# First norm of a decoder kernel by halves of the tokens, with weights ahead of x's second half, two tiles on the first half first, and the small vectors on ScalarE's queue

## What is computed

```python
def rms_norm(x, gain):
    xf = x.astype(jnp.float32)
    y = xf * lax.rsqrt(jnp.mean(xf * xf, axis=-1, keepdims=True) + NORM_EPS)
    return (y * gain.astype(jnp.float32)).astype(x.dtype)
...
h = rms_norm(x, mix_norm[layer])
...
q, k, v, g = jnp.split(h @ w_in, [H * dk, 2 * H * dk, 2 * H * dk + H * dv], axis=-1)
q = apply_rope(q.reshape(B, S, H, dk), positions)
k = apply_rope(k.reshape(B, S, H, dk), positions) * (dk ** -0.5)
```

## Time and profile before

| | us |
|---|---|
| median of 3 runs | 2768.65 (2768.4 to 2768.74) |
| the profiled execution, its device time | 2771.12 |
| span of its profile | 2769.2 |
| TensorE busy in the span | 2699.9 |
| VectorE / ScalarE / GpSimd busy | 1357.4 / 827.0 / 1268.4 |
| TensorE busy in the first 38 us | 20.77 |

### The profile page before, as it was taken

One profiled execution on the slowest core, in us unless ns is written; L12 is line 12 of the kernel. 1 busy time (PEld: TensorE's weight loads), 2 busy tenths in 40 slices (PEclk: granted clock), 3 DMA queues, 4 the chain that ended last, 5 costly groups with the idle time before them and its releaser, 6 DMA issues.

```text
span 2769.2 us, 35757 instructions
## 1 busy us (share of the span) xinstructions
PE 2699.9 (97%) x12145; PEld 2237.2 (81%) x12145; DVE 1357.4 (49%) x1866; ACT 827.0 (30%) x1404; POOL 1268.4 (46%) x1215
## 2 busy tenths in 40 slices
PE   7999999999999899999999999999988999999998
PEld 6888888888888788888888788787876888888886
DVE  7423423432334764454545537355577444545455
ACT  4220210120023523333323524324265222222223
POOL 3323323323322555665555445253445555655553
PEclk9999999999999999999999999999999999999999
DMA  3102102101111111111121111111111111111211
GB/s 134 39 31 65 42 31 66 46 31 58 50 35 46 33 59 49 53 45 49 53 64 53 31 50 47 31 58 39 47 50 33 56 53 53 45 45 56 65 53 76
DMA packets 173483, 140.03 MB, mean 51 GB/s; under 512 B 8657, under 2 KB 142929, under 8 KB 173393
## 3 DMA queue, kind: packets, MB, share of 16 engines
q1 hardware_dynamic: 171664, 133.53, 15.6%
q10 hardware_dynamic: 1728, 5.26, 0.5%
HBM read 133.51 MB, written 5.24 MB: 50 GB/s over the span
## 4 chain that ended last, share of the span: by engine, by line
PE 91%; DVE 5%; ACT 2%; issue 1%; DMA 0%; POOL 0%; POOLq 0%; SPq 0%; DVEq 0%; ACTq 0%
PE ps L690 30%; PE ps L694 30%; PE ps L693 30%; DVE uc L1940 1%; PE ps L894 0%; PE ps L776 0%; DVE residual L1596 0%; DVE residual L1853 0%; DVE residual L2011 0%; DVE f_h_lo L1736 0%; DVE gate_buf L1945 0%; DVE xn L1552 0%; DVE h_sum_a L1725 0%; DVE uc L1935 0%; ACT L1465 0%
## 5 line engine op out<-in xcount | busy, mean ns | idle before, releaser
L527 POOL TENSOR_TENSOR f_w_lo<-f_raw,f_w_hi 128x512 fp32r<-128x512 f32 x262 | 340.7, 1303 | 434.4 <-ACT f_w_hi L1240 434.3
L690 PE MATMUL ps<-f_h_hi,f_w_hi 128*128 128x512 f32 x1232 | 483.2, 392 | 17.9 <-DVE f_h_lo L1725 12.1
L693 PE MATMUL ps<-f_h_lo,f_w_hi 128*128 128x512 f32 x1232 | 481.5, 391 | 0.0
L694 PE MATMUL ps<-f_h_hi,f_w_lo 128*128 128x512 f32 x1232 | 481.3, 391 | 0.0
L487 POOL TENSOR_TENSOR small<-w_raw 128x1 f32<-128x1 f32 x200 | 55.1, 275 | 845.2 <-PE ps L690 830.0
L1853 DVE TENSOR_TENSOR residual<-ps,residual 128x512 f32<-128x512 f32 x352 | 239.3, 692 | 160.0 <-PE ps L694 160.0
L690 PEld LDWEIGHTS ps<-f_h_hi,f_w_hi 128*128 128x128 f32 x1232 | 232.6, 189 | 70.0 <-issue 15.9
L1240 ACT ACTIVATE f_w_hi<-f_raw 128x512 fp32r<-128x512 f32 x262 | 164.4, 629 | 367.0 <-PE ps L694 349.6
L694 PEld LDWEIGHTS ps<-f_h_hi,f_w_lo 128*128 128x128 f32 x1232 | 232.6, 189 | 48.7
L693 PEld LDWEIGHTS ps<-f_h_lo,f_w_hi 128*128 128x128 f32 x1232 | 232.7, 189 | 48.1
L690 PE MATMUL ps<-f_w_hi,f_act_hi 128*128 128x512 f32 x688 | 268.0, 389 | 3.2 <-POOL f_last_lo L527 3.2
(11 more groups left out here) (261 smaller groups left out, 4773.9 us busy)
## 6 DMA issues: line engine op xcount, KB each, us to landing
f_raw<-in_ffn_w_gu SPq DMA_DIRECT2D x176, 256.0 KB, 3.4
w_raw<-in_ret_w_in SPq DMA_DIRECT2D x96, 256.0 KB, 2.8
f_raw<-in_ffn_w_down SPq DMA_DIRECT2D x88, 256.0 KB, 2.7
w_raw<-in_lru_w_in SPq DMA_DIRECT2D x48, 256.0 KB, 2.9
w_raw<-in_ret_w_out SPq DMA_DIRECT2D x32, 256.0 KB, 2.6
w_raw<-in_lru_w_out SPq DMA_DIRECT2D x24, 256.0 KB, 2.6
residual<-in_x SPq DMA_DIRECT2D x8, 512.0 KB, 6.6
out_y<-residual SPq DMA_DIRECT2D x8, 512.0 KB, 2.6
```

Of the source, the lines that this page charges most:

```text
L527: nc.gpsimd.tensor_tensor(lo, src, hi.bitcast(F32), ALU.subtract).then_inc(f_wready, 1)
L690: m = nc.tensor.matmul(o, l_hi, r_hi, start=start, stop=False, skip_group_check=onto)
L693: nc.tensor.matmul(o, l_hi, r_lo, start=False, stop=False, skip_group_check=onto)
L694: return nc.tensor.matmul(o, l_lo, r_hi, start=False, stop=stop, skip_group_check=onto)
```

## The change

The first norm gets functions of its own on each engine (`first_norm` on ScalarE and VectorE, `first_tiles` on TensorE). The other norms keep theirs, apart from renamed helpers.

- SP loads blocks 0 to 3 of x, the first three weight units (tile 0 and tile 1, features 0 to 511, then tile 0, features 512 to 1023), then blocks 4 to 7, positions and frequencies, then the rest.
- The seven small vectors are issued from ScalarE's queue, after a first square root on a dummy operand, which loads the table.
- The fourth weight unit is split into a buffer of its own, `w4_hi` and `w4_lo`, so POOL does not wait for a place in the ring.
- TensorE first transposes the small vectors. Then it works by halves of the tokens: transposes of k = 0 to 3 of the first half, then products of tiles 0 and 1 on it, with the transposes of k = 4 to 7 in between; then the same for the second half. Products of a tile and half go to bank tile + 2 * hf, transposes use banks 4 to 7.
- ScalarE and VectorE follow this order; VectorE scales blocks 0, 1, 2 and 4, 5, 6 for the lower features and 0, 1 and 4, 5 for the upper ones, ScalarE the others.

```diff
-            for s in range(SB):
-                sp.dma_start(X[:, s * D:(s + 1) * D], x[0, s * P:(s + 1) * P, :]).then_inc(x_in[s], 16)
-            vec = scr[:, 8 * 1024:8 * 1024 + P]
-            for at, n, src in ((C_MIX, 16, mix_norm.rearrange("l (k p) -> (l k) p", p=P)),
-                               (C_FFN, 16, ffn_norm.rearrange("l (k p) -> (l k) p", p=P)),
-                               (C_CONV, 48, lru_conv_w[0].rearrange("j (k p) -> (j k) p", p=P)),
-                               (C_CONVB, 12, lru_conv_b[0].rearrange("(k p) -> k p", p=P)),
-                               (C_BR, 12, lru_b_r[0].rearrange("b c -> (b c)").rearrange("(k p) -> k p", p=P)),
-                               (C_BI, 12, lru_b_i[0].rearrange("b c -> (b c)").rearrange("(k p) -> k p", p=P)),
-                               (C_LAM, 12, lru_lambda[0].rearrange("(k p) -> k p", p=P))):
-                sp.dma_start(vec[at:at + n, :], src).then_inc(vec_in, 16)
-            sp.dma_start(pos[:], positions.to_broadcast([P, S])).then_inc(pos_in, 16)
-            sp.dma_start(invf[:], inv_freq).then_inc(pos_in, 16)
-
+            def x_blocks(first, end):
+                for s in range(first, end):
+                    sp.dma_start(X[:, s * D:(s + 1) * D], x[0, s * P:(s + 1) * P, :]).then_inc(x_in[s], 16)
+            x_blocks(0, 4)
             def load(slot, src, ready):
...
+                    if first and j == RING:
+                        x_blocks(4, SB)
+                        sp.dma_start(pos[:], positions.to_broadcast([P, S])).then_inc(pos_in, 16)
+                        sp.dma_start(invf[:], inv_freq).then_inc(pos_in, 16)
                     if j < 8:
-                        tile, kh = j // 2, j % 2
+
+                        tile, kh = (j % 2, j // 2) if first and j < 4 else (j // 2, j % 2)
                         src = rows(ret_w_in[0], kh, (tile // 2) * D + h * DK + (tile % 2) * P)
...
-                    used = None if first and j < RING else u if j < 2 else u - 1
+                    used = None if first and j <= RING else u if j < 2 else u - 1
+                    if first and j == RING:
+                        place = w4_hi[:], w4_lo[:]
...
+            def first_tiles(u0):
+                e0 = JB_NORM[0]
+                def transposes(hf, ks):
+                    for k in ks:
+                        i = hf * KT + k
+                        if i >= 4:
+                            pe.wait_ge(psum_free, e0 + i - 3)
+                        if k % 4 == 0:
+                            pe.wait_ge(xn_dve, hf * 5 + (3 if k == 0 else 5))
+                            pe.wait_ge(xn_act, hf * 3 + (1 if k == 0 else 3))
+                        for s in range(4):
+                            c = (hf * 4 + s) * D + k * P
+                            m = nc.tensor.transpose(bank(4 + i % 4, s * P, P), xn[:, c:c + P], ident[:])
+                        m.then_inc(psum_full, 1)
+                def products(hf, j, kks=range(4)):
+                    tile, kh = j % 2, j // 2
+                    if hf == 0:
+                        pe.wait_ge(w_ready, u0 + j + 1)
+                    for kk in kks:
+                        k = kh * 4 + kk
+                        if tile == 0:
+                            pe.wait_ge(psum_free, e0 + hf * KT + k + 1)
+                        r = slice(k * S + hf * 512, k * S + (hf + 1) * 512)
+                        if j < RING:
+                            w = slice(j * 512 + kk * P, j * 512 + (kk + 1) * P)
+                            w_h, w_l = w_hi[:, w], w_lo[:, w]
+                        else:
+                            w_h, w_l = w4_hi[:, kk * P:(kk + 1) * P], w4_lo[:, kk * P:(kk + 1) * P]
+                        m = three(bank(tile + 2 * hf), w_h, w_l, h_hi[:, r], h_lo[:, r],
+                                  k == 0, k == KT - 1, hf == 1 and kk == 0)
+                        if hf and k == KT - 1:
+                            m.then_inc(psum_full, 2)
+                pe.wait_ge(ident_ready, 2)
+                pe.wait_ge(vec_in, 16 * 7)
+                nc.tensor.transpose(ps[:, 0:P], scr[:, 8 * 1024:8 * 1024 + P], ident[:]).then_inc(vec_T, 1)
+                transposes(0, range(4))
+                products(0, 0)
+                products(0, 1, (0, 1))
+                transposes(0, range(4, 8))
+                products(0, 1, (2, 3))
+                products(0, 2)
+                products(0, 3, (0,))
+                transposes(1, range(4))
+                products(0, 3, (1, 2, 3))
+                products(1, 0)
+                products(1, 1, (0, 1))
+                transposes(1, range(4, 8))
+                products(1, 1, (2, 3))
+                products(1, 2)
+                products(1, 3)
...
+            def first_norm():
+                def square(s):
+                    act.wait_ge(x_in[s], 16)
+                    square_rows(s, 0)
+                def scaled(s, half):
+                    c = s * D + half * 512
+                    nc.scalar.activation(xn[:, c:c + 512], X[:, c:c + 512], ACT.Copy,
+                                         scale=rstd[:, s:s + 1]).then_inc(xn_act, 1)
+                def upper(hf, ks):
+                    for k in ks:
+                        i = hf * KT + k
+                        full(JB_NORM[0] + i)
+                        nc.scalar.activation(h_hi[:, k * S + hf * 512:k * S + (hf + 1) * 512], bank(4 + i % 4),
+                                             ACT.Copy, scale=cols[:, C_MIX + k:C_MIX + k + 1]).then_inc(h_rounded, 1)
+                act.wait_ge(ident_ready, 2)
+                load_sqrt()
+                vec = scr[:, 8 * 1024:8 * 1024 + P]
+                for at, n, src in ((C_MIX, 16, mix_norm.rearrange("l (k p) -> (l k) p", p=P)),
+                                   (C_FFN, 16, ffn_norm.rearrange("l (k p) -> (l k) p", p=P)),
+                                   (C_CONV, 48, lru_conv_w[0].rearrange("j (k p) -> (j k) p", p=P)),
+                                   (C_CONVB, 12, lru_conv_b[0].rearrange("(k p) -> k p", p=P)),
+                                   (C_BR, 12, lru_b_r[0].rearrange("b c -> (b c)").rearrange("(k p) -> k p", p=P)),
+                                   (C_BI, 12, lru_b_i[0].rearrange("b c -> (b c)").rearrange("(k p) -> k p", p=P)),
+                                   (C_LAM, 12, lru_lambda[0].rearrange("(k p) -> k p", p=P))):
+                    act.dma_start(vec[at:at + n, :], src).then_inc(vec_in, 16)
+                for s in range(4):
+                    square(s)
+                root(0, 4, 1)
+                act.wait_ge(n_rstd, 1)
+                scaled(3, 0)
+                act.wait_ge(cols_ready, 1)
+                upper(0, (0, 1))
+                square(4)
+                upper(0, (2, 3))
+                scaled(2, 1)
+                scaled(3, 1)
+                square(5)
+                upper(0, (4,))
+                square(6)
+                upper(0, (5,))
+                square(7)
+                upper(0, (6, 7))
+                root(4, SB, 2)
+                act.wait_ge(n_rstd, 2)
+                scaled(7, 0)
+                upper(1, range(4))
+                scaled(6, 1)
+                scaled(7, 1)
+                upper(1, range(4, 8))
+            first_norm()
...
+            def first_norm():
+                def square(s):
+                    dve.wait_ge(x_in[s], 16)
+                    c = s * D + 512
+                    STT(scr[:, 2048 + s * 512:2048 + (s + 1) * 512], X[:, c:c + 512], 1.0, X[:, c:c + 512],
+                        ALU.mult, ALU.mult, accum_out=ssq[:, 8 + s:9 + s]).then_inc(n_sq_dve, 1)
+                def scaled(s, half):
+                    c = s * D + half * 512
+                    TS(xn[:, c:c + 512], X[:, c:c + 512], rstd[:, s:s + 1], None, ALU.mult).then_inc(xn_dve, 1)
+                def lower(hf, ks):
+                    for k in ks:
+                        i = hf * KT + k
+                        c = slice(k * S + hf * 512, k * S + (hf + 1) * 512)
+                        dve.wait_ge(h_rounded, i + 1)
+                        STT(h_lo[:, c], bank(4 + i % 4), cols[:, C_MIX + k:C_MIX + k + 1], h_hi[:, c].bitcast(F32),
+                            ALU.mult, ALU.subtract).then_inc(psum_free, 1)
+                for s in range(4):
+                    square(s)
+                inverse_root(0, 0, 4, 1)
+                for s in range(3):
+                    scaled(s, 0)
+                dve.wait_ge(vec_T, 1)
+                nc.vector.tensor_copy(cols[:], ps[:, 0:P]).then_inc(cols_ready, 1)
+                dve.wait_ge(cols_ready, 1)
+                lower(0, (0, 1))
+                square(4)
+                lower(0, (2, 3))
+                scaled(0, 1)
+                scaled(1, 1)
+                square(5)
+                lower(0, (4,))
+                square(6)
+                lower(0, (5,))
+                square(7)
+                lower(0, (6, 7))
+                inverse_root(0, 4, SB, 2)
```

(8 more changed lines are left out.)

84 lines of the change are left out of this document (30 added, 54 removed).

## The result

| | before | after |
|---|---|---|
| median of nine runs each, us | 2770.15 (2768.4 to 2771.55) | 2776.11 (2774.84 to 2779.2) |
| ratio, 95% interval | | 1.0023 (1.0015 to 1.0032) |
| profiled execution, device time (span) | 2771.12 (2769.2) | 2774.87 (2773.0) |

The change costs 6.0 us by the medians (4.2 to 8.9 by the interval), against a forecast of 3.1. The 2776.1 us lies inside the range given (2766 to 2776.5), but by the bound of 5.5 us that the prediction set between "same" and "slower" it is just "slower", and not clearly, since the interval reaches from 4.2 to 8.9. So the traces can explain 3.8 of the 6.0 us.

A forecast was written before the change was run, and what follows sets the result against it. TensorE, busy 97% of the span, was taken to bound the kernel, with VectorE's chain level at the first gate unit. VectorE's 1.6 us plus 1.5 us of slow clock gave +3.1 us, forecast 2771.8 us, range 2766 to 2776.5.

The forecast's parts named there:

- same: Outcome class for the total time: within 5.5 us (0.2%), what a measurement can tell from no change; chance 0.73.
- slower: Outcome class for the total time: more than 5.5 us lost; chance 0.21, from three quarters of C and 0.08 of the forecast.
- The mechanism: First gate unit: TensorE, 7.5 us ahead, waits 6.5 us for VectorE's later freeing of banks; chance 0.60.
- VectorE's chain: Rope tables to second rope pair: start +1.0, one more split +1.3, first pair -0.7; last bank freed 1.6 us later.
- The early table load: ScalarE's root in the first norm: load hidden, scaling starts at 9.9 in place of 10.93, 1.0 us won.
- Rival C, late small vectors: Start of first norm: vectors land at 14.4, TensorE's first instruction waits 3.2 us, total 2775.0 us; chance 0.17.
- A, level: Rival at the first gate unit: nothing lost, last bank freed within 1 us of today's, 2768.0 to 2769.6; chance 0.17.
- B, VectorE does not bind: Rival at the first gate unit: TensorE keeps its 7.5 us lead less 1 us of waits, 2762.2 us; chance 0.06.
- The first norm on TensorE: First transposes at 11.25, last four groups at 35.45, tile 1 ends at 44.0, TensorE some 7.5 us ahead.
- slow start: TensorE's first instructions in the first norm: slow pace until about 16.4, costing 2.6 us (bounds 1.8 and 4.2).
- The clock: Clock of 0.50 after TensorE's wait at the first gate unit, costing 1.5 us (bounds 0 and 3.4).
- Sum: Whole kernel: 1.6 us of VectorE's lateness plus 1.5 us of slow clock, +3.1 us; forecast 2771.8 us.

The follow-up runs named there:

- a_short: Changed kernel without the coarse pass of the angle reduction, 6 of the 17 rope table instructions; 2769.13 us, ratio 0.9994 to the kernel before.
- b_short: Kernel before without the coarse pass of the angle reduction, 6 of the 17 rope table instructions; 2770.97 us, ratio 1.0000 to the kernel before.
- b_vec: Kernel before with only the early table load and the small vectors from ScalarE's queue; 2770.44 us, ratio 0.9999 to the kernel before.
- a_xfirst: Changed kernel with all of x issued ahead of the weights in SP's queue; 2780.14 us, ratio 1.0033 to the kernel before.
- a_hold: Changed kernel with POOL's first split held until VectorE's three first scalings are done; 2775.27 us, ratio 1.0018 to the kernel before.
- a_splits: Changed kernel with weight units 4 and 5 split early into own buffers, VectorE waiting for tile 2 behind the tables; 2773.66 us, ratio 1.0013 to before.
- a_early: Changed kernel with the second-half transposes of k = 4 to 7 moved ahead of more products; 2775.73 us, ratio 1.0016 to the kernel before.
- a_early_mix: Changed kernel with a_early's order of transposes and seven table instructions moved into VectorE's idle places; 2765.75 us, ratio 0.9986 to the kernel before.
- a_best: Changed kernel with a_hold, a_splits, a_early and five table instructions moved into VectorE's idle places; 2766.97 us, ratio 0.9989 to the kernel before.
- a_warm: Changed kernel with six repeats of three matmuls in TensorE's wait at the first gate unit; 2775.71 us, ratio 1.0019 to the kernel before.

## Why the prediction was right or wrong

**The mechanism held.** The forecast said that TensorE would be some 7.5 us ahead and give all of it back at the bank that VectorE frees, because VectorE's chain would be later, not earlier. TensorE was 6.9 us ahead at the gate unit (66.39 against 73.27), waited 7.2 us there (1.36 + 0.39 + 4.66 + 0.74; forecast 6.5 in one piece), and VectorE's last freeing instruction ended 2.86 us later. The first 1.75 us are for banks of the first rope pair, which the forecast had free in time. a_short and b_short show that this chain, and not another, sets the end.

**The early table load: right in kind, half in size.** The load is hidden, as said. Scaling starts at 10.35, 0.58 earlier than before and not 1.0: block 3 of x landed 0.44 us later (8.79 against 8.35). The forecast costed the small vectors at nothing and kept the landing at 8.35. The other traces tell most of the cause. b_vec and a_xfirst, with the seven vectors on ScalarE's queue but all of x ahead of the weights, have block 3 at 8.63 and 8.62; b_short, with neither, at 8.27; after and its other variants, with both, at 8.64 to 8.83. So some 0.3 us came with the vectors and at most 0.2 with the weights.

**Rival C, late small vectors, is refuted.** They landed by 9.54, 4.6 us after the last of their issues was done (4.57 + 0.39), and TensorE then waited for the scalings until 12.70. *A, level*, fell with the 2.86 us, and *B, VectorE does not bind*, with the 4.66 us wait. The Trainium skill (DMA: Bandwidth & Descriptors, "Issuing engines are not separate DMA queues") has transfers of different issuers interleave; this landing, in the middle of x's, agrees.

**The first norm on TensorE: 0.6 us too short.** Full transposes start at 12.70, not 11.25. Of the 1.45 us, 1.0 is the split beside the scalings (shown by a_hold; the forecast took 0.5 later in the sum) and 0.45 the landing. The slow start cost less than taken (about 2 us by the starts of the first transposes and products, an estimate; forecast 2.6), so tile 3 ended at 66.39 against 65.8, and the last transposes ran at 35.97 against 35.45.

**VectorE's chain: the step that failed.** The forecast had +1.0 - 0.7 + 1.3 = +1.6; the trace has +2.86. The tables start 1.66 us later (39.97 against 38.31), 0.67 more than taken. The first pair takes 10.07 us, 1.5 less than before (11.57), where 0.7 less was taken. And the tables take 23.3 us, not 21.9. This last is the term that was mis-sized. Its price per split was near: 23.3 less 15.5 of undisturbed work is 7.8 us, for six splits 1.3 each. (The 15.5 adds up durations; by the distance from start to start, 1.26 us for the long ones and about 0.74 for the others, undisturbed work is 16.2, and a split costs 1.1 us before, 1.2 here, and 1.4 in a_splits and a_early.) The count was wrong: I moved the splits earlier and arrived at five. The first of the six starts at 39.63, just as the tables do, since TensorE had run ahead and released it, and the last at 61.38. Two more splits, not one: +2.7, not +1.3. Taking three out gave 1.0 us each (a_splits). The count alone does not settle it, though: in a_early the tables met five and took 23.05 us, 2.5 more than before. Which instructions a split lies beside counts as well, and the two were not separated. What the count missed is in the starts: the first three are 2.7 us apart (39.63, 42.34, 45.06), the others 5.44. A place in the ring comes free when TensorE begins a unit, and by halves it reuses the four units of tiles 0 and 1 in a second pass, where a unit lasts four products, 12 x 0.227 = 2.7 us. So the splits were not only earlier but also closer together, and just at the tables' start.

**The clock: half of what was taken.** 0.50 came as said, from 74.9 to 81.7, but most of it lay in the wait. Its cost was 0.8 us (lag 3.60 against 2.80 with the clock kept up), where I took 1.5 with bounds of 0 and 3.4. The Trainium skill (TensorE: Matmul & The Clock Gate, "Terms") would price the stretch at half of itself, 3.4 us; the runs show less, since the time in which TensorE waits anyway costs nothing at any clock.

**Sum.** VectorE's chain was 1.3 us too early in the forecast and the clock 0.8 us too dear, so that most of the two errors cancelled; that the sum came out near is luck in part. By its own terms the trace gives +2.86 + 0.74 = +3.60 where the forecast had +3.1, and +3.76 at the end of the span. Two things outside it make up the rest of the distance to 2776.1. The median that I started from, 2768.65 of three runs, became 2770.15 over nine: 1.5 us. And the medians differ by 6.0 where the profiled pair differs by 3.8. Where those 2.2 us lie is not shown, since a trace stands for one execution. What the runs give is a hint only: three of the four runs of after above its median have a mean granted clock of 0.991, and all four below it 0.992 or 0.993. The 96 runs of the kernel before beside the experiments (median 2770.6) point the same way: the 14 at 0.992 have a mean of 2773.1 us, the 37 at 0.994 one of 2770.1. That longer half clocks at later norms make the 2.2 us is thus likely, but it stays open. These 1.5 and 2.2 us are most of the distance between 2771.8 and 2776.1; the tables, the step that failed, are the largest error among the terms.

**The chances.** "Slower" had 0.21, of which 0.13 stood for a rival that did not occur. It was reached on the main path, with 2.9 us more than forecast and a bound of 5.5 us between "same" and "slower". A forecast of +3.1 with such terms and a start from three runs should have put more there.

## What to carry to other kernels

When one engine is sped up ahead of a point where two chains meet, first work out how early the other chain can be, and count the disturbances that follow the faster engine into the other's work: here the tables met two more weight splits and took 2.7 us longer, and a lead of 6.9 us became a loss. Move work of the slower chain into its own idle places before, or together with, the change that makes the other faster; a_early_mix kept 5.1 us of lead that way. When a collision is moved into a buffer of its own, look at what the buffer makes others wait for (2.8 us in a_best). And price a slow clock only where TensorE has work that nothing else holds up.

## What the runs showed of the hardware that was not expected

- **The half clock had few lengths.** In all these traces a stretch at 0.50 lasted 3.4, 6.8 or 10.2 us, but for the last one of each, which runs into the end of the program. Which of them it was changed between kernels at the same norm: near 1580 us, for example, 3.4 us in before and 6.8 in a_short. A lead or lag of a few microseconds made in the first head was changed by 0.2 to 3.5 us by the end of the program (table of lags). On this kernel an edit in one stage can be judged by the lag behind it sooner than by the total time.
- **Matmuls that do nothing kept the clock up.** 18 repeated matmuls in a wait of 4.7 us kept it at 1.00 and took 0.8 us off the lag, 21 in a_early 1.3. The total time of a_warm does not show it.
- **The clock column hides the slow start.** It says 1.00 for the first 38 us of after, while sixteen transposes from 12.70 took 3.67 us and sixteen from 28.03 took 1.94. The spacing between starts has to be read there.
- **Splits on POOL disturb VectorE's SBUF work, and not its reading of PSUM.** Three scalings of 1.28 us took 2.29 beside one split, and a split in the tables cost 1.1 to 1.4 us by starts. In after the split from 67.00 to 69.11 lay beside four rope instructions that read a tile from PSUM, and each took its usual 0.68 us; in a_splits the split at 67.56 lay beside two that read SBUF alone, and they took 0.94 and 1.78 us instead of 0.68.
